# Two layers written out instead of looped, with another order of the first loads and of the first norm

## What is computed

```
for i in range(2):
    x = x + 0.5 * swiglu(rms_norm(x, ffn1_norm[i]), w_gate, w_up, w_down)   # inner width 2816
    z = rms_norm(x, mix_norm[i]) @ w_in[i]
    y_a = dilated_attention_mixture(q, k, v)   # three groups of four heads, from z
    y_b = spatial_gating(gelu(u), gelu(v))     # chunks of 128 tokens
    y_c = multiscale_pool(z[...])              # trailing means over 2, 4, 8, 16 tokens
    x = x + (sum of sigmoid gates from z times the projected branches) @ w_out[i]
    x = x + 0.5 * swiglu(rms_norm(x, ffn2_norm[i]), ...)
return rms_norm(x, final_norm)
```

## Time and profile before

| | us |
|---|---|
| median of the runs (3) | 2360.91 |
| profiled execution, its own time | 2360.02 |
| its span, first to last instruction | 2358.3 |
| PE busy | 2343.2 |
| DVE busy | 1083.1 |
| ACT busy | 706.9 |

### The profile page before, as it was taken

One profiled execution on the slowest core, in us unless ns is written; L12 is line 12 of the kernel. 1 busy time (PEld: TensorE's weight loads), 2 busy tenths in 40 slices (PEclk: granted clock), 3 DMA queues, 4 the chain that ended last, 5 costly groups with the idle time before them and its releaser, 6 DMA issues.

```text
span 2358.3 us, 27546 instructions
## 1 busy us (share of the span) xinstructions
PE 2343.2 (99%) x11021; PEld 1937.6 (82%) x11021; DVE 1083.1 (46%) x1031; ACT 706.9 (30%) x652; POOL 27.4 (1%) x58
## 2 busy tenths in 40 slices
PE   8999999999999999999999999999999999999999
PEld 6888888887888888888878888889878888888887
DVE  6444435455543644443354443365554455444433
ACT  4222222323522322222232222233344233222222
POOL 4000000000000000000000000000000000000000
PEclk9999999999999999999999999999999999999999
DMA  5223234322223332233322322332212332323221
GB/s 162 89 89 107 80 98 127 92 72 64 76 80 100 110 107 89 89 103 98 102 91 89 107 89 98 98 112 81 81 50 77 102 111 90 107 89 107 90 95 66
DMA packets 231340, 221.82 MB, mean 94 GB/s; under 512 B 4208, under 2 KB 229600, under 8 KB 231264
## 3 DMA queue, kind: packets, MB, share of 16 engines
q1 hardware_dynamic: 225744, 215.29, 29.1%
q10 hardware_dynamic: 5520, 5.51, 0.7%
HBM read 218.69 MB, written 2.10 MB: 94 GB/s over the span
## 4 chain that ended last, share of the span: by engine, by line
PE 97%; DVE 2%; issue 0%; DMA 0%; ACT 0%; SPq 0%; DVEq 0%
PE psum L452 83%; PE psum L657 6%; PE psum L591 2%; PE side L675 1%; PE side L704 1%; PE side L452 1%; PE psum L462 1%; DVE rstd L1193 1%; DVE w_lo L1120 0%; PE side L691 0%; PE side L686 0%; PE side L601 0%; DMA raw<-in_ffn_w_gate_dram 0%; PE side L573 0%; PE side L475 0%
## 5 line engine op out<-in xcount | busy, mean ns | idle before, releaser
L452 PE MATMUL psum<-h_hi,w_hi 128*128 128x512 f32 x1968 | 769.3, 391 | 0.7 <-DVE w_lo L1120 0.7
L452 PE MATMUL psum<-h_hi,w_lo 128*128 128x512 f32 x1968 | 765.8, 389 | 2.1 <-issue 2.1
L452 PE MATMUL psum<-h_lo,w_hi 128*128 128x512 f32 x1968 | 765.7, 389 | 0.0
L1120 DVE TENSOR_TENSOR w_lo<-raw,w_hi 128x2048 fp32r<-128x2048 f32 (+2 forms) x223 | 468.4, 2100 | 339.8 <-ACT w_hi L786 339.1
L786 ACT ACTIVATE w_hi<-raw 128x2048 fp32r<-128x2048 f32 (+2 forms) x223 | 392.0, 1758 | 604.3 <-PE psum L452 581.1
L452 PEld LDWEIGHTS psum<-h_hi,w_hi 128*128 128x128 f32 x1968 | 369.5, 188 | 81.8 <-issue 3.7
L452 PEld LDWEIGHTS psum<-h_lo,w_hi 128*128 128x128 f32 x1968 | 369.5, 188 | 77.7 <-issue 1.4
L452 PEld LDWEIGHTS psum<-h_hi,w_lo 128*128 128x128 f32 x1968 | 369.4, 188 | 77.0
L452 PE MATMUL psum<-act_hi,w_hi 128*128 128x512 f32 x704 | 273.9, 389 | 0.0
L452 PE MATMUL psum<-act_hi,w_lo 128*128 128x512 f32 x704 | 273.9, 389 | 0.0
L452 PE MATMUL psum<-act_lo,w_hi 128*128 128x512 f32 x704 | 273.9, 389 | 0.0
(11 more groups left out here) (207 smaller groups left out, 1915.0 us busy)
## 6 DMA issues: line engine op xcount, KB each, us to landing
raw<-in_ffn_w_up_dram SPq DMA_DIRECT2D x44, 1024.0 KB, 5.3
raw<-in_ffn_w_gate_dram SPq DMA_DIRECT2D x43, 1024.0 KB, 5.4
raw<-in_w_in_dram SPq DMA_DIRECT2D x42, 1024.0 KB, 5.3
raw<-in_ffn_w_down_dram SPq DMA_DIRECT2D x32, 1024.0 KB, 4.9
raw<-in_ffn_w_down_dram SPq DMA_DIRECT2D x16, 768.0 KB, 4.2
raw<-in_w_in_dram SPq DMA_DIRECT2D x24, 512.0 KB, 4.5
raw<-in_w_out_dram SPq DMA_DIRECT2D x8, 1024.0 KB, 5.0
raw<-in_w_proj_b_dram SPq DMA_DIRECT2D x8, 512.0 KB, 3.5
```

The lines of the kernel that those rows point to most:

```text
L452: mm = nc.tensor.matmul(dst[:, c * S:(c + 1) * S], l[:, a], r[:, b], start=first and k == ks[0] and n == 0, stop=last and k == ks[-1] and ...
L1120: nc.vector.tensor_tensor(w_lo[s][:, a], raw[s][:, a], w_hi[s][:, a].bitcast(F32), ALU.subtract).then_inc(split_made, 1)
```

## The change

Five edits are in it. (1) The layer loop becomes a Python loop, so both layers stand in each engine's program, and the Ifs are decided when the program is built; the inner loops stay. (2) ACT issues x's four parts and the four quarters of the first weight unit in turn, x first; SP no longer issues the quarters, and waits for x's third part before it loads the second unit. (3) The gains of the first norm (16 rows) have a semaphore of their own; PE turns them alone behind x's first part, and turns all vectors a second time behind the first unit, into another bank, from where ACT copies the rest of the table. (4) PE turns x's third part behind the first quarter instead of ahead of it; ACT instead of DVE copies x's second part to xT; ACT's first steps are in another order, with all squares at the end. (5) The pause in `columns` is at pair 6 instead of 4, in every FFN.

```diff
@@ -96,11 +96,9 @@
...
-    UNITS_PER_LAYER = 2 * (2 * FF_UNITS + D_PAIRS * 3) + 6 + GROUPS + 7 + 6 * D_PAIRS + D_PAIRS
-
-    EV0, EV1 = 56, 52
+
     DOWN_K = [(k, min(k + UNIT_K, KF)) for k in range(0, KF, UNIT_K)]
-    assert (S, D, TILES, RES, KD, DEPTH) == (4 * P, 8 * P, 4, 4, 8, 2) and len(DOWN_K) == 3 and UNITS_PER_LAYER % 2 == 0
+    assert (S, D, TILES, RES, KD) == (4 * P, 8 * P, 4, 4, 8) and len(DOWN_K) == 3
     assert FF % UNIT_N == 0 and D_PAIRS == 4 and BW == 2 * UNIT_N == S
@@ -185,6 +183,7 @@
...
         N_VEC = T_CSCALE + DEPTH * KB
+        GAINS = DEPTH * KD
         assert N_VEC <= P
@@ -199,6 +198,7 @@
...
         first_h = sem("first_h")
+        gains_loaded = sem("gains_loaded")
         vectors_turned = sem("vectors_turned")
@@ -287,7 +287,7 @@
...
                     src = vec.rearrange("l k p -> (l k) p")
-                sp.dma_start(vectors[row:row + src.shape[0], :], src).then_inc(vectors_loaded, 16)
+                sp.dma_start(vectors[row:row + src.shape[0], :], src).then_inc(gains_loaded if vec is ffn1_norm else vectors_loaded, 16)
                 row += src.shape[0]
@@ -319,14 +319,12 @@
...
-            sp.wait_ge(split_made, counts["split_made"].next())
-            for q in range(D_PAIRS):
-                a = slice(q * 2 * UNIT_N, (q + 1) * 2 * UNIT_N)
-                sp.dma_start(raw[0][:, a].rearrange("p (k n) -> p k n", n=UNIT_N),
-                             view(ffn1_w_gate, 0, 0, UNIT_N, 2 * q, 2 * q + 2)).then_inc(first_loaded[q], 16)
+
+            counts["split_made"].next()
+            sp.wait_ge(x_loaded[2], 16)
             load.slot = 1
-            with rounds(sp, DEPTH, counts, split_made=UNITS_PER_LAYER) as layer:
+            for layer in range(DEPTH):
                 load_ffn(layer, ffn1_w_gate, ffn1_w_up, ffn1_w_down, 1)
@@ -355,8 +353,8 @@
...
                 load_ffn(layer, ffn2_w_gate, ffn2_w_up, ffn2_w_down, 0)
-                with sp.If(layer < DEPTH - 1):
-                    load([view(ffn1_w_gate, DEPTH - 1, 0, UNIT_N)])
+                if layer < DEPTH - 1:
+                    load([view(ffn1_w_gate, layer + 1, 0, UNIT_N)])
@@ -406,7 +404,7 @@
...
-                pool.wait_ge(side_evacuated[1], 3 + layer * 4)
+                pool.wait_ge(side_evacuated[1], 4 + layer * 4)
@@ -444,7 +442,7 @@
...
                         need(k)
-                    if at == 4 and pause:
+                    if at == 6 and pause:
                         pause()
@@ -521,14 +519,14 @@
...
             turn_in(0, begin_side(0))
-            pe.wait_ge(vectors_loaded, 16 * 6)
-            nc.tensor.transpose(psum[0][:, 0:N_VEC], vectors[0:N_VEC, :], ident[0:N_VEC, 0:N_VEC]).then_inc(vectors_turned, 1)
+            pe.wait_ge(gains_loaded, 16)
+            nc.tensor.transpose(psum[0][:, 0:GAINS], vectors[0:GAINS, :], ident[0:GAINS, 0:GAINS]).then_inc(vectors_turned, 1)
             turn_in(1, begin_side(1))
-            turn_in(2, begin(1))
             pe.wait_ge(table_made, 1)
...
                 if q == 1:
+                    turn_in(2, begin(1))
@@ -544,10 +542,10 @@
...
             mm.then_inc(unit_done, 1)
-
-            with rounds(pe, DEPTH, counts, unit=UNITS_PER_LAYER, ev0=EV0, ev1=EV1,
-                        sv0=8 + ATT, sv1=4, h=3 * D_PAIRS, acc=3 * (1 + KD), act=2 * FF_UNITS, w_sT=1, pooled=4,
-                        vb=1, p=ATT, pT=PAIRS, head=PAIRS, y=2, merged=D_PAIRS) as layer:
+            pe.wait_ge(vectors_loaded, 16 * 5)
+            nc.tensor.transpose(begin_side(1)[:, 0:N_VEC], vectors[0:N_VEC, :], ident[0:N_VEC, 0:N_VEC]).then_inc(vectors_turned, 1)
+
+            for layer in range(DEPTH):
                 ffn()
@@ -738,11 +736,8 @@
...
                 ffn()
-                with pe.If(layer < DEPTH - 1):
+                if layer < DEPTH - 1:
                     open_ffn()
-
-            counts["ev0"].next(-1)
-            counts["h"].next(-D_PAIRS)
@@ -853,22 +848,25 @@
...
-                            with act.If(layer < DEPTH - 1):
+                            if layer < DEPTH - 1:
                                 split()
...
                 if last:
-                    with act.If(layer < DEPTH - 1):
+                    if layer < DEPTH - 1:
                         split()
...
                               x[0].rearrange("(t p) n -> p t n", p=P)[:, :, d * UNIT_N:(d + 1) * UNIT_N]).then_inc(x_loaded[d], 16)
+                act.dma_start(raw[0][:, d * 2 * UNIT_N:(d + 1) * 2 * UNIT_N].rearrange("p (k n) -> p k n", n=UNIT_N),
+                              ffn1_w_gate[0].rearrange("(k p) n -> p k n", p=P)[:, 2 * d:2 * d + 2, 0:UNIT_N]
+                              ).then_inc(first_loaded[d], 16)
             act.wait_ge(vectors_turned, 1)
-            nc.scalar.activation(table[:, 0:N_VEC], psum[0][:, 0:N_VEC], ACT.Copy).then_inc(table_made, 1)
+            nc.scalar.activation(table[:, 0:GAINS], psum[0][:, 0:GAINS], ACT.Copy).then_inc(table_made, 1)
             act.wait_ge(table_made, 1)
@@ -892,29 +890,28 @@
...
             first_input(0, 1)
-            for d in (1, 2):
-                first_input(d, 0)
-                first_input(d, 1)
-                first_weights(d)
-            taken(2)
-            square(0, squares[0])
+            first_input(1, 0)
+            first_input(1, 1)
+            first_weights(1)
+            keep(1, side_evacuated[1])
+            first_weights(2)
+            first_input(2, 0)
+            first_input(2, 1)
+            first_weights(3)
             first_input(3, 0)
             first_input(3, 1)
-            first_weights(3)
             keep(2, evacuated[1])
...
             keep(3, side_evacuated[0])
-            taken(3)
-            square(1, squares[1])
-            taken(1)
-            square(2, squares[2])
-            taken(2)
-            square(3, squares[3])
-
-            with rounds(act, DEPTH, counts, unit=UNITS_PER_LAYER, raw0=8 * UNITS_PER_LAYER + 16 * 2,
-                        raw1=8 * UNITS_PER_LAYER + 16 * 3, ev0=EV0, ev1=EV1, se0=8 + ATT, act=2 * FF_UNITS,
-                        sd0=7 + PAIRS, sd1=4, ln=1, yb=2, neg=ATT, pT_written=ATT, head=ATT, merged=D_PAIRS) as layer:
+            for d, t in enumerate((2, 3, 1, 2)):
+                taken(t)
+                square(d, squares[d])
+            act.wait_ge(vectors_turned, 2)
+            nc.scalar.activation(table[:, GAINS:N_VEC], side[1][:, GAINS:N_VEC], ACT.Copy).then_inc(side_evacuated[1], 1)
+            act.wait_ge(side_evacuated[1], counts["se1"].next())
+
+            for layer in range(DEPTH):
                 ffn(layer, layer * KD + T_MIX, False)
@@ -1220,7 +1217,7 @@
...
                         if end and last:
-                            with dve.If(layer < DEPTH - 1):
+                            if layer < DEPTH - 1:
                                 split()
@@ -1265,7 +1262,7 @@
...
             first_weights(1)
-            side_out(1, nc.vector.tensor_copy(pair(xT, 1), side[1][:, :]))
+            counts["se1"].next(2)
             first_input(4)
@@ -1289,11 +1286,7 @@
...
-            chained = sum(w.bit_length() for w in POOL_WINDOWS) + 5 + D_PAIRS + ATT
-            with rounds(dve, DEPTH, counts, unit=UNITS_PER_LAYER, hi=UNITS_PER_LAYER, ev0=EV0, ev1=EV1, step=chained,
-                        h_hi=12, sq=12, acc=3 * (1 + KD), side0=7 + PAIRS, scored_b=PAIRS, half=6, side1=4, se0=8 + ATT, se1=4, std=3, rstd=3, silu=2 * FF_UNITS,
-                        act_hi=2 * FF_UNITS, gelu=2, ln_std=1, yc_hi=2, yb_hi=2, y=2, pooled=KB, exp=ATT,
-                        head=PAIRS, gate=3 * D_PAIRS, merged=D_PAIRS) as layer:
+            for layer in range(DEPTH):
                 ffn(layer, layer * KD + T_MIX, False)
```

## The result

The changed kernel takes 2365.01 us (median of 20 runs, 2364.17 to 2365.86) against 2360.8 us before (20 runs); the ratio is 1.0018, 95% interval 1.0011 to 1.0024. It is 4.2 us slower, where 0.8 us were forecast, and 0.4 us outside the stated range. The profiled execution took 2364.39 us, its span is 2362.7 us, 4.4 us over that of before.

What follows compares the result with a forecast made beforehand. TensorE, busy for 2343.2 of 2358.3 us, was taken as the bound. The terms -2.24 - 0.5 + 4.08 - 0.55 gave +0.8 us, 2361.7 us on the median, range 2357.3 to 2364.6.

Steps and rivals of the forecast that it cites:

- Step 1: Layer loop written out: PE's stall at the first layer's end goes, -2.24 us; register operations in the norm chains, -0.5 us.
- Rival D: Second layer: straight code is fetched late once there too, so the 2.24 us come back; 2363.9 us, chance 0.09.
- Step 2: Pause from place 4 to 6: norm sums 1.36 us later in three later FFNs, +4.08 us; first FFN unchanged.
- Step 3: Kernel start: acc of the first norm ready about 0.5 us earlier, taken as -0.55 us; bounds -1.2 and +3.1.
- so 4.4 us to 5.2: Start, ACT's queue: eight transfer issues instead of four take 4.4 us and end at 5.2, table load ending before.
- Rival E: Start: ACT's eight transfers block its queue longer; at 1 us each ACT starts 2.5 us late; 2364.2 us, chance 0.05.
- The copy of the rest of the table ... 0: First norm on ACT: the 0.3 us copy stands behind the squares, before a root at about 30, costing 0.
- Net 0: First FFN: six matmuls fill the wait for acc but are missing behind the norm sums; next unit's start unchanged.
- Rival C: Start: PE's first matmuls run at the lower clock level, +3.1 instead of -0.55 us; 2365.3 us, chance 0.11.

Runs made afterwards that it cites:

- the quarters on SP: Changed kernel with pause at place 4 and ACT's table wait at the first residual, plus SP issuing the four weight quarters behind the gains: 2356.78 us, ratio 0.9984.
- the version from what was learnt: Kernel before with layers written out, gains alone first, first quarter behind them on SP, table wait at first residual, pause at 4, later FFNs 3: 2353.55 us.
- pause 4 with the later wait: Changed kernel with the pause at place 4 in every FFN and ACT's wait for the table's rest moved to the first residual: 2358.12 us, ratio 0.9988.
- pause 4: Changed kernel with the pause at place 4 again in every FFN: 2359.65 us, ratio 0.9996.
- pause 6 in the first FFN: Changed kernel with the pause at place 6 in the first FFN alone and at 4 in the three later ones: 2360.27 us, ratio 0.9998.
- third part of x first: Changed kernel with pause at 4 and table wait at the first residual, plus x's third part turned ahead of the first quarter: 2357.11 us, ratio 0.9988.

## Why the prediction was wrong

**Step 1, layers written out, was right.** The gap of 2.24 us went as a whole, and nothing came in its place; the register operations gave 0.1 us per chain. Rival D did not come. What the Trainium skill ("Runtime: NRT & Kernel Launch", section "Instruction fetch mechanics") says of sequential prefetch and of taken branches agrees with this: the second layer's straight code runs without such a gap.

**Step 2, the later pause, was right for the three later FFNs:** 1.36 us each, as the kernel with that edit alone shows, 4.1 us.

**Step 3, the start, failed, and with it the part of step 2 on the first FFN.** The start was taken at -0.55 us and cost 3.6 us on the trace, 3.3 by the medians. That alone explains the miss: with +3.6 in the place of -0.55 the sum would be 4.9 us, with +3.3 4.6, against 4.2 measured. Four parts were wrong:

- "so 4.4 us to 5.2": eight issues took 6.1 us. The last two were not 0.55 but 1.4 us each. Rival E named this and priced it for all eight; the first copy did come 1 us earlier when this was undone, and the medians gave 1.3 us, less than they can show.
- "The copy of the rest of the table ... 0": the copy does cost nothing, but the wait behind it does, 1.3 us. I counted what the wait waits for, and not what it does to the table load that had stood hidden in front of the root. With the fall of the clock that it brought about it is the largest term, 2.8 us when undone, and it was nowhere in my list.
- "Net 0" for the pause in the first FFN (it stands in step 2): about true for the sum of the two waits, and it left out the clock. With the late root, PE idled for 2.8 us in one stretch, the clock fell, and 1.6 us went there. Moved back, the pause gains only about 0.6 us in this FFN, as the other stretch (2.2 us) brought the fall too. Without the table load's 1.3 us the stretch was 1.4 us, and the profiled execution kept its clock.
- Rival C looked for the lower level at PE's first matmuls. The trace has it there: the first 12 take from 10.83 to 14.88 us, 4.05 instead of 2.7. It moved x's third part; that this moved acc is argued, not shown. That is half of C's mechanism, but not its price: the whole effect on acc, with the late queue, is 0.9 us instead of -0.5. That C's time, 2365.3 us, lies 0.3 us from the measured one is chance: most of the real loss came by the table load and by a fall of the clock 30 us later.

The Trainium skill ("TensorE: Matmul & The Clock Gate", Part 1) calls the lower level the state after idling. I had applied it to the start alone. The trace of the norm agrees with it: behind 2.8 us without a matmul, those up to 44.08 us started up to 0.43 us apart. To see that beforehand, the late table load had to be seen first.

Up to its last transpose the end of the kernel gave 0.7 us to the changed one, in which the transposes behind the last wait ran longer at the upper level (granted 0.69 in 2353 to 2358.2 us, against 0.56 before in the same stage). In the 14 profiled executions this stage, from the last down-projection matmul to the last transpose, took 9.5 to 11.5 us, while its program differs by register operations at most. It goes with the moment at which the clock falls: 7.8 us behind that last matmul in the shortest (the quarters on SP), 5.2 us behind it in the longest (the version from what was learnt).

What stays open: how much of the 0.9 us on acc belongs to the queue and how much to the order of turning. Undone one at a time, they gave 1.3 and 1.0 us by the medians, within what the times can tell; both together were not run on that kernel. The 0.9 us itself is of one execution. In the five traces with this start acc is ready at 28.74 to 30.27 us, in the five with the old one at 28.7 to 28.8: the new start is later on the whole, and much less steady.

## What to carry to other kernels

A wait costs what it puts in order, not only what it waits for: look for a table load, or other work the engine does ahead, that stands behind it. When an edit is argued as neutral because it moves idle time from one place to another, add up the longest stretch that it leaves: here one of 2.8 us cost 1.6 us more by TensorE's clock, and one of 1.4 us did not. An edit in a shared helper is to be priced at each place where it is called: here it could help the first of four norms at best, did nothing for it, and lost 1.36 us in each of the others. And the value of an earlier start is read at the next thing that waits (acc), not at the first instruction that moves.

## What the runs showed of the hardware

- A jump back to far code cost PE 2.24 us (2.65 in the kernel with pause 6 alone), and only where the layer's end was not straight code. The jump took 3.49 us in the sequencer and was covered; two instruction blocks were brought in that stretch, and PE stood eight matmuls into the new round.
- Two waits in front of an ACTIVATE with another function table: one of them, the wait for DVE, became an instruction of its own, and the table load (1.28 us) ran behind it, on the path. With one wait the load ran ahead, while the ACTIVATE waited.
- The first six issues in ACT's queue took 0.48 to 0.63 us each, the seventh and eighth 1.52 and 1.25 us. SP's queue issued ten transfers in a row at 0.33 to 0.65 us each (the quarters on SP).
- In the first 60 us PE's granted clock fell to 0.5 for 3.4 us at idle stretches of 2.0, 2.2, 2.8 and 2.8 us (pause 4 with the later wait, pause 4, pause 6 in the first FFN, the changed kernel). With stretches of 1.3 to 1.8 us, and with one of 2.0 us (third part of x first), it did not in the executions profiled. In the kernel with pause 4 and the later wait the time differed by 3.5 us from run to run.
